# Expert blocks in four 32-column tiles, turns on VectorE, gather behind scatter: a four-layer mixer stack with a mixture of experts

## Chip, cores and metric

One NeuronCore of a Trainium2 chip. The metric is the device time of one launch in microseconds (us), all weights in HBM at its start. Everything is float32.

## The reference, cut to what matters

The program is a stack of mixer layers (attention, latent attention, mLSTM, a hybrid layer) over 256 tokens of width 1024, and behind them a layer of routed experts. Only that last layer is touched by the change:

```python
def clamped_swiglu(hgu):
    gate, up = jnp.split(hgu, 2, axis=-1)
    gate = jnp.minimum(gate, SWIGLU_LIMIT)
    up = jnp.clip(up, -SWIGLU_LIMIT, SWIGLU_LIMIT)
    return gate * jax.nn.sigmoid(SWIGLU_ALPHA * gate) * (up + 1)

# routed_moe: 256 tokens, 32 experts, top 4 of them for each token
top_v, top_e = lax.top_k(xt @ w_router + b_router, TOP_K)
gates = jax.nn.softmax(top_v, axis=-1)
# the 1024 assignments are sorted by expert; each expert gets blocks of 64 slots
def expert_block(args):
    xb, e = args                                  # 64 x 1024
    return clamped_swiglu(xb @ w1[e] + b1[e]) @ w2[e] + b2[e]   # w1: 1024x2048, w2: 1024x1024
# y[token] += gate * yb[slot];  x = x + gate2 * y;  the output is rms_norm(x, final_norm_w)
```

## The kernel before

The experts' weights are 12 MB each: eight chunks of 1 MB of w1 (128 input features each, c = 0 to 7) and four of w2 (c = 8 to 11). `expert_weights` in SBUF holds exactly 12 chunks. SyncE (SP) issues all loads (L2066): chunk c of the next expert goes out when the semaphore `used` says that the last block of the present expert is done with its chunk c. Ahead of chunk 0 goes the load of the next expert's bias (`load_bias1`, L2795), which waits for `bias_used` of that last block.

An expert with more than 64 assignments has two or more blocks. There are 36 blocks for 32 experts; a plan, made on VectorE while block 0 runs (`sort_and_plan`), orders the experts, and the blocks from 3 on are a hardware loop (`Fori`) on each engine.

One block i on PE (TensorE): `first_products` (L3060) multiplies the 64 gathered rows `xt` with w1, gate half into PSUM bank 4 and up half into bank 5. The 64 slots fill 64 of the array's 128 columns, so two tiles run side by side, g = 0 on output features 0 to 511 and g = 1 on 512 to 1023. After chunk 3 stands the gather of block i+1 (`gather`, L3032: a matrix `pick` of ones times the normalised tokens `htok`, into bank 6). Then `scatter_last` (L3045): the output of block i-1, `ys`, times `spread`, which holds the gates by token, is added to the sums in banks 0 to 3. Then `second_products`: four transposes of the activation on PE (L3098), four of the gathered rows (`turn_gathered`, L3040), a wait for ScalarE's copy `at_` (L2923), and the products with w2 (L3108) into bank 7. Each matmul call is two matmul instructions, each with a weight load, in the trace; a transpose is one.

ScalarE (ACT): `copy_gathered` (L2900), `sigmoid` (L2919), the copy of the turned activation (L2923), and `copy_turned`, eight activations that apply the layer's scale and shift and write `xt` (L2906).

VectorE (DVE) in one block: `activation` (L3312 to L3319), `gates_of_slots` (L3325, `eq2`: which slot is which token, times its gate; L3329), `lay_bias` (four shuffles, L3183) for block i+1, `spread_slots` (L3332, a sum over 128x1024), `tables` (L3243 to L3248, the `pick` of a later block), and `outputs` (L3337), which copies bank 7 to `ys` and waits for the end of the second products.

At the end PE scatters the last block (two calls, one for each half of the tokens), and ScalarE and VectorE normalise and scale (L2938, L3370) before the stores.

## Time and profile before

| | |
|---|---|
| time, three runs | 2301.73, 2302.03, 2305.65 us (median 2302.03) |
| profiled execution | span 2306.2 us; of what lies around the span the page tells nothing |
| PE busy | 2209.2 us, 96% |
| VectorE busy | 1194.8 us, 52% |
| ScalarE busy | 650.0 us, 28% |
| read from HBM | 567.46 MB |
| TensorE clock, mean | 0.993 of full speed |

Busy PE time is the time in which at least one matmul is under way; matmuls overlap, and a matmul in another tile of the array runs at the same time. The chain of waits follows the last instruction back to what released it; a transfer is in it with the whole time from its issue to its landing, queueing behind other transfers included. The expert layer runs from about 1310 us to the end.

### The profile page before, as it was taken

To read this page: it belongs to the slowest core of one execution; us is meant where nothing else is said; L and a number is where in the kernel's file an instruction comes from. 1 tells how busy PE (TensorE), PEld (TensorE's weight loads), DVE (VectorE), ACT (ScalarE), POOL (GpSimd) and SP (SyncE) were. 2 spreads that over 40 slices of the span, in tenths; PEclk is the share of its full clock that TensorE was granted. 3 is DMA by queue.
4 is the path that set the end of the run, shared out by engine and by line. 5 is a ranking of instruction groups with operands and counts; after the bars stand their busy time and mean duration, and the time that the engine had idled before them with its cause. 6 is when DMAs were issued, how large, how long until landed. Compare 5 with 4: busy or idle time off the path is not lost. (4 is left out here: it accounts for less than half of the span.)

```text
span 2306.2 us, 29645 instructions
## 1 busy us (share of the span) xinstructions
PE 2209.2 (96%) x10363; PEld 1188.4 (52%) x10364; DVE 1194.8 (52%) x2716; ACT 650.0 (28%) x1658; POOL 101.8 (4%) x234
## 2 busy tenths in 40 slices
PE   8999899999999999999999899999999999999997
PEld 3546685478744578777878633333333323333332
DVE  4989468453895563636745453334343333334334
ACT  3018442443221363336333321111111111111112
POOL 0001000000000051002001000000000000000000
PEclk9999999999999999999999999999999999999999
DMA  9670035301477103331241599989989998998998
GB/s 398 250 291 34 1 146 191 110 1 45 175 266 278 39 2 110 110 110 38 74 147 37 231 373 421 421 357 421 422 365 422 421 421 366 421 421 366 421 421 335
DMA packets 110280, 569.68 MB, mean 247 GB/s; under 512 B 11857, under 2 KB 13649, under 8 KB 51441
## 3 DMA queue, kind: packets, MB, share of 16 engines
q1 hardware_dynamic: 110192, 568.54, 61.6%
q8 instruction: 52, 0.85, 0.2%
q14 instruction: 36, 0.29, 0.0%
HBM read 567.46 MB, written 1.05 MB: 247 GB/s over the span
## 5 line engine op out<-in xcount | busy, mean ns | idle before, releaser
L3060 PE MATMUL PS<-BIG,PW 128*64 128x512 f32 x2304 | 514.1, 594 | 15.3 <-DMA BIG<-in_w 14.7
L3060 PEld LDWEIGHTS PS<-BIG,PW 128*64 128x64 f32 x2304 | 161.6, 137 | 353.6 <-issue 301.9
L3312 DVE TENSOR_SCALAR PW<-PS 128x512 f32<-128x512 f32 x36 | 24.9, 692 | 494.6 <-PE PS L3060 494.6
L3108 PE MATMUL PS<-BIG,PW 128*64 128x512 f32 x1152 | 255.4, 595 | 8.6 <-ACT PW L2923 8.6
L386 DVE SCALAR_TENSOR_TENSOR BIG<-BIG,COND_ROWS 128x1024 f32<-128x1024 f32 x128 | 153.4, 1221 | 24.9 <-DMA BIG<-in_w_ada_columns 24.6
L3108 PEld LDWEIGHTS PS<-BIG,PW 128*64 128x64 f32 x1152 | 79.2, 137 | 161.0 <-issue 142.7
L2900 ACT COPY BIG<-PS 128x512 f32<-128x512 f32 x37 | 21.7, 586 | 486.6 <-PE PS L3032 486.6
L1148 PE MATMUL PS<-HT,BIG 128*128 128x512 f32 (+1 forms) x448 | 152.0, 501 | 0.0
L1148 PEld LDWEIGHTS PS<-HT,BIG 128*128 128x128 f32 x448 | 85.1, 190 | 65.3 <-issue 60.3
L658 PE MATMUL PS<-HT,BIG 128*128 128x256 f32 x512 | 111.6, 379 | 1.4 <-PEq L863 1.4
L1553 PE MATMUL PS<-BIG,HT 128*128 128x512 f32 x256 | 110.0, 592 | 0.0
L658 PEld LDWEIGHTS PS<-HT,BIG 128*128 128x128 f32 x512 | 97.1, 190 | 14.9 <-issue 1.8
L386 DVE SCALAR_TENSOR_TENSOR PW<-BIG,COND_ROWS 128x1024 f32<-128x1024 f32 x80 | 97.5, 1219 | 11.4 <-ACT COND_ROWS L1169 5.0
L2906 ACT ACTIVATE PW<-PS,MOD,GAIN 128x64 f32<-128x64 f32 x296 | 91.9, 423 | 0.7 <-PE PS L3040 0.7
L2919 ACT ACTIVATE PW<-PW 128x512 f32<-128x512 f32 x36 | 22.7, 630 | 225.6 <-DVE PW L3312 225.1
L993 DVE TENSOR_REDUCE ST<-PS 128x2 f32<-128x1024 f32 (+1 forms) x64 | 65.5, 1023 | 34.8 <-PE PS L1413 32.2
L1553 PEld LDWEIGHTS PS<-BIG,HT 128*128 128x128 f32 x256 | 48.6, 190 | 61.2 <-issue 61.2
L924 ACT ACTIVATE PW<-PS,ST 128x512 f32<-128x512 f32 (+1 forms) x128 | 77.3, 615 | 9.3 <-DVE ST L999 4.8
L3045 PE MATMUL PS<-PW,HT 64*128 64x512 f32 x288 | 72.9, 625 | 0.9 <-DVE PW L3337 0.9
L886 PE MATMUL PS<-CONST,PW 128*128 128x128 f32 x416 | 61.2, 286 | 11.4 <-DVE PW L1012 11.4
L937 ACT COPY PW<-PS 128x512 f32<-128x512 f32 (+1 forms) x128 | 58.7, 509 | 44.2 <-PE PS L886 43.6
L3032 PE MATMUL PS<-BIG,HT 128*64 128x512 f32 x296 | 69.9, 593 | 1.0 <-DVE HT L3237 1.0
(547 smaller groups left out, 3171.6 us busy)
## 6 DMA issues: line engine op xcount, KB each, us to landing
BIG<-in_w SPq DMA_DIRECT2D x384, 1024.0 KB, 16.1
BIG<-in_l_w_ada_columns SPq DMA_DIRECT2D x40, 1024.0 KB, 7.2
BIG<-in_l_w_in SPq DMA_DIRECT2D x19, 2048.0 KB, 8.5
BIG<-in_w_ada_columns SPq DMA_DIRECT2D x24, 1024.0 KB, 7.1
BIG<-in_l_w_out SPq DMA_DIRECT2D x8, 2048.0 KB, 8.5
BIG<-in_w_in SPq DMA_DIRECT2D x7, 2048.0 KB, 8.1
BIG<-in_l_w_ada SPq DMA_DIRECT2D x4, 2048.0 KB, 17.9
BIG<-in_w_out SPq DMA_DIRECT2D x2, 2048.0 KB, 7.8
```

The lines of the kernel that those rows point to most:

```text
L386: ins = nc.vector.scalar_tensor_tensor(w if s else PRODUCTS, w, 1.0, COND_ROWS[:, row, :], ALU.mult, ALU.mult, accum_out=modulation(l)[:, ...
L658: ins = nc.tensor.matmul(PS[:, j % 4, 0:LAT], w[:, k, (m % 4) * P:(m % 4 + 1) * P], ot[:, k, s * LAT:(s + 1) * LAT], start=(k == 0), stop= ...
L886: ins = nc.tensor.transpose(PS[:, 4 + h, j * P:(j + 1) * P], probs[:, i % 2, h, kt * P:(kt + 1) * P], ident)
L924: nc.scalar.activation(probs[:, i % 2, h, a:b], PS[:, 2 * (i % 2) + h, a:b], ACT.Exp, bias=nm[:, i % 2, h:h + 1], scale=scale, accum_out=d ...
L993: dve_chain.link(dve, nc.vector.tensor_reduce(mx[:, i % 2, 0:2], s[:, :, a:b], AX, ALU.max))
L1148: ins = nc.tensor.matmul(PS[:, j % 4, 0:tok], *ops, start=(k == 0), stop=(k == KT - 1))
L1553: ins = nc.tensor.matmul(o, HT[:, k, m[1] * P:(m[1] + 1) * P], w[:, k, :], start=(k == 0), stop=(k == KT - 1))
L2906: nc.scalar.activation(xt[:, k % 4, k // 4, :], turned[:, k % 4, k // 4, :], ACT.Identity, bias=shift[:, k, :], scale=gained[:, k, :]).the ...
L3032: ins = nc.tensor.matmul(PS[64 * g:64 * g + 64, 6, :], pick[:, a, :], htok[:, a, g * 512:g * 512 + 512], start=(a == 0), stop=(a == 1))
L3045: ins = nc.tensor.matmul(PS[:, 2 * a + g, :], spread[64 * g:64 * g + 64, a * P:(a + 1) * P], ys[64 * g:64 * g + 64, :], start=False, stop= ...
L3060: ins = nc.tensor.matmul(PS[64 * g:64 * g + 64, 4 + half, :], xt[:, c % 4, c // 4, :], W[:, c, half * F + g * 512:half * F + g * 512 + 512 ...
L3108: ins = nc.tensor.matmul(PS[64 * g:64 * g + 64, 7, :], at_[:, k % 4, k // 4, :], W[:, 8 + k // 2, k % 2 * D + g * 512:k % 2 * D + g * 512 ...
```

## The change

A block keeps its 64 slots but is worked on as two parts u = 0, 1 of 32 slots. A part fills 32 columns, so four tiles run side by side, each with 256 output features; a chunk and half takes eight matmul calls of 256 columns where it took two of 512. Gather and second products are cut in the same way. The scatter becomes four row tiles of 32 slots. The output sums in banks 0 to 3 are laid out by feature quarter for it, and the two scatters at the end signal once, after the second.

The activation and the gathered rows are turned by VectorE (`nc.vector.transpose`, which turns each 32x32 block) in place of eight PE transposes and two ScalarE copies. The gather moves from inside the first products to behind the scatter. Since `spread` needs the two parts apart, VectorE does `eq2` and the sum over 128x1024 twice in each block; its `turn_gathered` stands ahead of them, and in front of the sort in block 0. The bias row for an expert is 8 KB in place of 16.

```diff
                     def scatter(a):
-                        for g in range(2):
-                            ins = nc.tensor.matmul(PS[:, 2 * a + g, :], spread[64 * g:64 * g + 64, a * P:(a + 1) * P],
-                                                   ys[64 * g:64 * g + 64, :], start=False, stop=False, skip_group_check=True)
+                        for u in range(2):
+                            for g in range(4):
+                                ins = nc.tensor.matmul(PS[:, g, a * 256:a * 256 + 256], spread[rows_of(g), u, a * P:(a + 1) * P],
+                                                       ys[rows_of(g), u * 256:u * 256 + 256], start=False, stop=False, tile_position=(PART * g, 0),
+                                                       skip_group_check=True)
                         return ins
...
                             for half in range(2):
-                                for g in range(2):
-                                    ins = nc.tensor.matmul(PS[64 * g:64 * g + 64, 4 + half, :], xt[:, c % 4, c // 4, :],
-                                                           W[:, c, half * F + g * 512:half * F + g * 512 + 512], start=False, stop=(c == 7),
-                                                           skip_group_check=True)
+                                columns = W[:, c, half * F:half * F + F].rearrange("p (k q x) -> p k q x", q=4, x=64)
+                                for u in range(2):
+                                    for g in range(4):
+                                        ins = nc.tensor.matmul(part_of(4 + half, g, u).rearrange("p (k x) -> p k x", x=64), xt[:, u, c, :],
+                                                               columns[:, :, g, :], start=False, stop=(c == 7), tile_position=(0, PART * g),
+                                                               skip_group_check=True)
...
                     def second_products(i, load, beside=None):
-                        pe.wait_ge(loop["act_ready"], i + 1)
-                        for j in range(4):
-                            cols = slice(j // 2 * 2 * P + j % 2, (j // 2 + 1) * 2 * P, 2)
-                            ins = nc.tensor.transpose(PS[:, 7, j * P:(j + 1) * P], act_[:, cols], ident)
-                        ins.then_inc(loop["act_turned"], 1)
-                        turn_gathered(i + 1)
-                        pe.wait_ge(loop["act_copied"], i + 1)
+                        pe.wait_ge(loop["act_turned"], i + 1)
...
                     with pe.Fori(3, n) as i:
                         load = pe.value_load(plan[0:1, bass.ds(i, 1)], min_val=0, max_val=E - 1)
-                        products_and_gather(i, load)
+                        first_products(i, load)
                         scatter_last(i)
+                        gather_next(i)
                         second_products(i, load)
                     pe.wait_ge(loop["spread_ready"], n)
                     pe.wait_ge(loop["y_copied"], n)
-                    for a in range(2):
-                        scatter(a).then_inc(ending["tile_scattered"], 1)
+                    scatter(0)
+                    scatter(1).then_inc(ending["tiles_scattered"], 1)
...
+                    def turn_gathered(i):
+                        dve.wait_ge(loop["gathered"], i + 1)
+                        nc.vector.transpose(xturned, PS[:, 6, :].rearrange("p (u k r) -> p u k r", u=2, r=PART)).then_inc(loop["gather_turned"], 1)
+
...
                     ts(first_blocks, blocks[:, 0:1], -1.0, None, ALU.add).then_inc(loop["first_blocks_ready"], 1)
+                    turn_gathered(0)
...
                         nc.vector.scalar_tensor_tensor(act_, up, 1.0, sig, ALU.add, ALU.mult).then_inc(loop["act_ready"], 1)
+                        dve.wait_ge(loop["act_ready"], i + 1)
+                        nc.vector.transpose(at_.rearrange("p u (k j) s -> p (u k) j s", j=2), act_.rearrange("p (k r j) -> p k j r", r=PART, j=2)).then_inc(loop["act_turned"], 1)
...
+                    def spread_slots(i):
+                        dve.wait_ge(steps, i * 10 + 7)
+                        nc.vector.tensor_reduce(spread[:, 0, :], eq2.rearrange("p k t -> p t k"), AX, ALU.add).then_inc(steps, 1)
+                        dve.wait_ge(steps, i * 10 + 8)
+                        gates_of_slots(1)
+                        dve.wait_ge(steps, i * 10 + 9)
+                        nc.vector.tensor_reduce(spread[:, 1, :], eq2.rearrange("p k t -> p t k"), AX, ALU.add).then_inc(loop["spread_ready"], 1)
                         nc.vector.tensor_scalar(slot, slot, float(SLOT), None, ALU.add).then_inc(steps, 1)
...
                     with dve.Fori(1, n) as i:
                         activation(i)
-                        gates_of_slots(i, load_of(i + 1))
+                        load = load_of(i + 1)
+                        turn_gathered(i + 1)
+                        dve.wait_ge(bias_landed, load * 16 + 16)
+                        gates_of_slots(0)
                         lay_bias()
                         dve.wait_ge(loop["scattered"], i)
-                        spread_slots()
-                        dve.wait_ge(loop["gathered"], i + 2)
-                        tables(lambda x: i * 8 + (8 + x))
+                        spread_slots(i)
+                        tables(lambda x: i * 10 + (10 + x))
                         outputs(i)
```

In the code before block 1's loop, `turn_gathered(1)` stands behind VectorE's four copies of `drow` and `grow` (L3347) and ahead of `gates_of_slots(0)` and `lay_bias()`.

## Rows read from the trace of the kernel before

**Rows 1.** The page's chain that ended last, by engine.

```profile
PE 31%; DMA 7%; DVE 3%; SPq 2%; ACT 1%; issue 1%; ACTq 0%; DVEq 0%
```

**Rows 2.** Windows: us, busy us (instructions) of each engine, PEclk, DMA share, GB/s.

```profile
1926.00:2102.00 176.00, 169.89 (x792) 58.75 (x790) 63.23 (x134) 27.14 (x71) 0.00 (x0) 1.00 1.01 421
2102.00:2114.00 12.00, 12.00 (x58) 3.98 (x57) 5.73 (x14) 2.14 (x8) 0.00 (x0) 1.00 0.44 156
```

**Rows 3.** Chain that ended last, 1820 to 2306: start us, us, what.

```profile
1909.29 1.96 PE PS L3060 x8
...
2096.33 1.96 PE PS L3060 x8
...
2101.81 7.09 PE PS L3108 x32
```

**Rows 4.** SP: two loads in time order; waits of its queue (total, times, longest).

```profile
1359.84 22.71 SPq L2066 DMA_DIRECT2D BIG<-in_w  x12
...
2110.81 24.67 SPq L2066 DMA_DIRECT2D BIG<-in_w  x12
...
SPq L2795 <- DVE PS L3183: 81.1, 4, 22.2
```

**Rows 5.** Timeline of PE near the program's start: four 32-column tiles.

```profile
34.87 1.94 PE L314 MATMUL PS<-BIG,COND 128*32 128x256 f32 x32
```

**Rows 6.** Timeline of one block in the loop, PE and DVE.

```profile
1533.06 1.99 PE L3045 MATMUL PS<-PW,HT 64*128 64x512 f32 x8
...
1534.51 0.69 DVE L3319 SCALAR_TENSOR_TENSOR PW<-PW 128x512 f32<-128x512 f32 x1
...
1536.67 7.09 PE L3108 MATMUL PS<-BIG,PW 128*64 128x512 f32 x32 [0.24 <-ACT PW L2923]
...
1543.59 7.04 PE L3060 MATMUL PS<-BIG,PW 128*64 128x512 f32 x32
```

**Rows 7.** Groups by form, DVE, 1510 to 2280: busy us, mean ns | idle before.

```profile
L3183 DVE STREAM_SHUFFLE PS<-BIG 128x256 f32<-128x256 f32 x116 | 41.8, 423 | 0.0
L3325 DVE SCALAR_TENSOR_TENSOR HT<-HT,SM 128x1024 f32<-128x1024 f32 x29 | 37.2, 1284 | 2.1
```

**Rows 8.** PE's sequencer at a loop top: ns min/median/max, first and last start us.

```profile
L3165 PEldq ALU_OP  x1: 32/32/32, 1539.3 to 1539.3; - x1
...
L3057 PEldq FUSED_REGOPS  x1: 37/37/37, 1540.7 to 1540.7; - x1
```

**Rows 9.** Timeline of block 0, 1318 to 1347.

```profile
1321.97 0.15 DVE L3256 TENSOR_SCALAR SM<-SM 128x1 int32<-128x1 f32 x1
...
1323.07 0.59 ACT L2900 COPY BIG<-PS 128x512 f32<-128x512 f32 x1 [3.11 <-PE PS L3032]
...
1326.78 0.43 PE L3123 MATMUL PS<-PW,CONST 32*128 32x64 f32 x2
...
1346.81 3.65 PE L3108 MATMUL PS<-BIG,PW 128*64 128x512 f32 x16 [0.24 <-ACT PW L2923]
```

**Rows 10.** Timeline of the last block and the ending.

```profile
2290.25 1.94 DVE L3332 TENSOR_REDUCE HT<-HT 128x256 f32<-128x1024 f32 x1
...
2293.48 0.58 DVE L3248 TENSOR_REDUCE HT<-PW 128x64 f32<-128x256 f32 x1
2295.94 0.69 DVE L3337 TENSOR_TENSOR PW<-PS,BIG 128x512 f32<-128x512 f32 x1 [1.87 <-PE PS L3108]
2296.78 1.99 PE L3045 MATMUL PS<-PW,HT 64*128 64x512 f32 x8 [0.89 <-DVE PW L3337]
2297.94 0.60 ACT L2938 ACTIVATE PW<-PS 128x512 f32<-128x512 f32 x1 [5.30 <-PE PS L3045]
```

**Rows 11.** DMA by queue: of 1500 to 2290, of all; issues with us to landing.

```profile
q1 hardware_dynamic: 44626, 319.54, 97.6%
...
q8 instruction: 52, 0.85, 0.2%
...
out<-BIG SPq DMA_DIRECT2D x4, 256.0 KB, 2.2
```

More of the change, by code:

```diff
@@ L3106, in second_products @@
                                 pe.wait_ge(chunk_landed[8 + k // 2], load * 16 + 16)
-                            for g in range(2):
-                                ins = nc.tensor.matmul(PS[64 * g:64 * g + 64, 7, :], at_[:, k % 4, k // 4, :],
-                                                       W[:, 8 + k // 2, k % 2 * D + g * 512:k % 2 * D + g * 512 + 512], start=(k == 0),
-                                                       stop=(k == KT - 1))
+                            for u in range(2):
+                                for g in range(4):
+                                    ins = nc.tensor.matmul(part_of(7, g, u), at_[:, u, k, :],
+                                                           W[:, 8 + k // 2, k % 2 * D + g * 256:k % 2 * D + g * 256 + 256],
+                                                           start=(k == 0 and u == 0), stop=(k == KT - 1), tile_position=(0, PART * g),
+                                                           skip_group_check=True)
                             if k % 2 == 1:
@@ L3150, in _ @@
                     load = pe.value_load(plan[0:1, 1:2], min_val=0, max_val=E - 1)
-                    products_and_gather(1, load)
+                    first_products(1, load)
                     scatter_last(1)
+                    gather_next(1)
                     second_products(1, load)
                     load = pe.value_load(plan[0:1, 2:3], min_val=0, max_val=E - 1)
-                    products_and_gather(2, load)
+                    first_products(2, load)
                     pe.wait_ge(loop["bias2_scaled"], 1)
                     for a in range(2):
-                        for g in range(2):
-                            nc.tensor.matmul(PS[:, 2 * a + g, :], gates_by[0:E, a * P:(a + 1) * P], bias2[0:E, g * 512:g * 512 + 512],
-                                             start=False, stop=False, skip_group_check=True)
+                        for g in range(4):
+                            ins = nc.tensor.matmul(PS[:, g, a * 256:a * 256 + 256], gates_by[0:E, a * P:(a + 1) * P], bias2[0:E, g * 256:g * 256 + 256],
+                                                   start=False, stop=False, skip_group_check=True)
+                    ins.then_inc(loop["bias2_added"], 1)
+                    pe.wait_ge(loop["bias2_added"], 1)
                     scatter_last(2)
+                    gather_next(2)
                     second_products(2, load)
@@ L3306, in _ @@
                                                 ALU.add).then_inc(loop["gates_spread"], 1)
-                    dve.wait_ge(loop["gathered"], 1)
                     tables(lambda x: x)
@@ L3321, in load_of, with gates_of_slots @@
                     def load_of(i):
                         return dve.value_load(plan[0:1, bass.ds(i, 1)], min_val=0, max_val=E - 1)
-                    def gates_of_slots(i, load=None):
-                        nc.vector.scalar_tensor_tensor(eq2, drow, slot, grow, ALU.is_equal, ALU.mult).then_inc(steps, 1)
-                        dve.wait_ge(steps, i * 8 + 7)
-                        if load is not None:
-                            dve.wait_ge(bias_landed, load * 16 + 16)
+                    def gates_of_slots(u):
+                        nc.vector.scalar_tensor_tensor(eq2, drow, slot[:, u:u + 1], grow, ALU.is_equal, ALU.mult).then_inc(steps, 1)
@@ L3347, in _ @@
                             nc.vector.tensor_copy(flat(dst[:, 2 * h:2 * h + 2, :]), PS[:, 4 + h, :]).then_inc(loop["places_copied"], 1)
+                    turn_gathered(1)
                     dve.wait_ge(loop["places_copied"], 4)
+                    gates_of_slots(0)
                     lay_bias()
-                    gates_of_slots(0)
-                    spread_slots()
+                    spread_slots(0)
                     dve.wait_ge(loop["gains_copied"], 2)
                     outputs(0)
-                    dve.wait_ge(loop["gathered"], 2)
-                    tables(lambda x: 8 + x)
+                    tables(lambda x: 10 + x)
                     dve.wait_ge(*at("late_loaded", 32))
```

108 lines of the change are left out of this document (50 added, 58 removed).

## The prediction

> **What bounds the kernel now.** I read the page's chain of waits first. It puts 31% of the span on PE and 7% on DMA [rows 1], so a reader would look to TensorE. The windows say otherwise for the expert loop. Over 1926 to 2102 the 16 DMA engines are full (share 1.01, 421 GB/s), and behind it lies a short hole (2102 to 2114 at 0.44) [rows 2]. There are four such holes, one where an expert needs two blocks: there SP also waits for VectorE before the bias load, four times [rows 4]. The two blocks of such an expert use one set of weights, so no slot of the 12 MB ring comes free until the second block has used its chunk 0.
>
> A cycle from hole to hole is 7 blocks and 6 experts: chunk 0 of A, the first block of a two-block expert, is past when PE waits for its chunk 7, at 2096.33, and the matching point of the cycle before is 1909.29, 187.0 us earlier [rows 3]. Six experts are 6 x 12 x 1.049 MB = 75.5 MB, at 421 GB/s 179.3 us; the other 7.7 us are the hole. PE's own period is 26.1 us a block (first products to first products), 182.6 for seven: PE has 4.4 us a cycle to spare, 0.6 a block, and beyond 187.0 / 7 = 26.7 us a block it would become the bound. So work taken off PE is given back as waiting for chunks. What counts is three places: the hole, the start of the stream, and the tail after the last chunk.
>
> **The hole, before.** PE waits for chunk 7 of A (landing at x = 2096.33), multiplies it in 1.96, and starts the second products at 2101.81, x + 5.48. They take 7.09; then chunk 0 of block B is multiplied and SP issues the next load at 2110.81, x + 14.5 [rows 3, 4]. All of that is in front of the DMA's restart.
>
> **The change on that path.** (1) *Matmuls.* A two-tile pair moves 2 x 512 columns, four tiles 4 x 256: equal work. Eight two-tile matmuls of a chunk take 1.96 [rows 3]; 32 four-tile ones of 256 columns, a form the kernel already has at its start, take 1.94 for the work of a chunk [rows 5]. So first products 13.8, gather 1.8 and second products 7.0 stay as they are, at 0.054 us a matmul where it was 0.22. The scatter as four row tiles of 32 is shown nowhere. Two row tiles of 64 run at full overlap (8 in 1.99) [rows 6], so I take 1.84 and keep 3.5 (two at a time) as the other end.
>
> The Trainium skill (TensorE: Matmul & The Clock Gate, Back-to-back issue gap) gives about 81 ns a matmul as the sustained floor of load and matmul pairs at 128 columns. By it the 448 matmuls of a block would take 36 us and not 24. The trace's row, 61 ns each with the tail of the last one in it, does not bear it out for four tiles.
>
> (2) *Order.* Before, scatter (1533.06), wait, four turns of the activation, four of the gathered rows, ACT's copy, second products at 1536.67: 3.6 us from scatter to second products [rows 6]. After: scatter 1.84, gather 1.84, 3.7 us together. Beside it VectorE ends its last product at 1535.20 and turns it; the turn of 128x512 is bounded by a 128x512 product (0.69) and by a 128x1024 strided sum scaled to 512 (1.94 in [rows 10], half is 0.97) [rows 6]. I take 0.69: the shuffle, the nearest operation, takes 0.42 for 256 columns [rows 7]. Ready at 1536.0 or 1536.3, before PE comes at 1536.8. So the four turns, the copy and their waits leave PE (some 1.8 us a block), the gather takes their place, and second products start 0.1 later relative to x: 4 x 0.1 = +0.4 over four holes. In the plain blocks PE's period falls from 26.1 to about 24.5, and that buys nothing.
>
> (3) *Loop top.* PE's sequencer does the branch, the read of the expert number and the waits from 1539.3 to 1540.7, 1.4 us, while PE still has work up to 1543.59 [rows 6, 8]. That lead, 4.3 us, is some 19 matmuls and their loads at 0.22. After the change 19 matmuls last 19 x 0.054 = 1.05. If the lead is a number of instructions, PE idles 1.4 - 1.05 = 0.4 at each loop top, one of which lies in each hole: 4 x 0.4 = +1.6. Bounds: 0 (a deeper queue), and 1.4 each, 5.6 (no lead).
>
> (4) *Bias.* Its load halves to 8 KB; for the second block it has landed, and xt and the bias are ready about 3.5 us after the second products begin, against 7: hidden. The cover gone, each us late would cost as much in each hole.
>
> **The start.** Block 0 [rows 9]: the gather's ACT copy (from 1323.07) and the four turns become one VectorE turn, so block 0 starts some 0.6 earlier. But `turn_gathered(0)` stands in front of the sort on VectorE and waits for the gather (its queue is free at 1322.1, the gather ends at 1323.05, the turn 0.7 later): the sort comes 1.7 later. PE asks for it at 1326.78 only, after chunk 0, so part of that is free; I leave 0.9 as delay, between none and the whole 1.7. Before the second products of block 0 (1346.81) turns and copy are gone, as in every block: of the 1.8 there I count 1.4 here, since less PE work stands between. Net -0.5. The stream becomes full when SP issues chunk 0 of expert 2 at 1359.84 [rows 4], 3.9 after the end of these second products, and moves with them: -0.5. Block 1 waits for `turn_gathered(1)`, which stands behind four copies on VectorE, some 0.9 us; its chunk 0 is done at 1358.5, before SP asks. Bounds -1.5 and +1.5 (the sort's delay kept whole). ACT's eight row copies of 256 for four of 512 end 0.3 later, in front of nothing.
>
> **The tail.** After the last chunk nothing hides anything. Before, VectorE was done with its tables at 2294.06, and `outputs` started when PE ended, 2295.94 [rows 10], 7.14 after the second products began. After, VectorE waits for the gather (S + 0.25, S the start of the second products), and then has in front of `outputs`: turn 0.65, eq2 1.2, four shuffles 1.35, sum 1.94, eq2 1.42, sum 1.94, slot 0.1, tables 1.95 [rows 7, 10] = 10.55. `outputs` starts at S + 10.7, not 7.14: +3.5. (In other blocks y is needed only at the next scatter, S + 21: hidden.) Then the ending waits for both scatters and not one: 1.16 from the scatter's start to ACT's first square before [rows 10], 2.05 after: +0.9. Tail +4.4; the bounds are 3.9, and 5.5 with the slow turn twice and a slower scatter's 1.6 apart.
>
> **Sum.** -0.5 + 0.4 + 1.6 + 4.4 = +5.9. The page gives 2306.2 as span of the profiled execution, 4.2 over the median of the runs, 2302.03; from 2306.2 the sum is 2312.1, and I carry the difference to the median: 2307.9, say 2308. A change under 0.2%, 4.6 us, is about what cannot be told from none.
>
> **Rivals.**
> *No idle at the loop top, no change.* The queue is deep enough, or the start gives 1.5: +3 to +4.3, 2305 to 2306.3, within 0.2%. For it: the lead is seen only in time, not as a count. 0.24.
>
> *PE was the bound after all, faster.* The chain's 31% on PE [rows 1] would then be real and 1.1 to 1.6 us a block be saved: 33 x 1.1 = -36, 2270. Against it stands a DMA share of 1.01 over 170 us at a stretch. Together with smaller gains in the holes (a scatter and gather that overlap): 0.09.
>
> *The loop outgrows instruction memory, clearly slower.* PE's loop has 248 instructions now (64, 32, 8 and 8 matmuls, 112 in all, as many loads, turns, control) and about 920 after (448 matmuls). In the loop before, the only queue that moves is the data's; in the whole program instruction packets of queue 8 number 52, of 0.85 MB, 16 KB each [rows 11]. If a branch back then waits for such a packet, the smallest transfers land in 2.2 us [rows 11]: 4 x 2.2 = 9 in the holes, and PE's period 24.9 + 2.2 = 27.1 passes 26.7, where it becomes the bound: 0.4 x 33 = 13 more instead of idle. About +20 to +25, 2325 to 2330. Below a stall of 1.8 only the holes pay. How many such packets PE keeps, no row shows. The Trainium skill (Runtime: NRT & Kernel Launch, Instruction fetch mechanics) speaks both ways: 128 KiB for PE, which would hold the loop, and a window of two 16 KiB pages outside of which a taken branch stalls. With it goes the case that four-tile matmuls in long runs take more than 60 ns each (26.7 us / 448), from which point PE decides too: at 70 ns a block takes 31.4, and 4.7 x 33 = 155 us are added. Both together 0.10.
>
> *Main case*, 2306.7 to 2316 (the latter with the slow scatter, 1.6 in four holes and in the tail): 0.57.
>
> **Numbers.** Slower 0.57 + 0.10 = 0.67; within 0.2% 0.24; faster 0.09. Range 2302 to 2316: it leaves out the faster case and the fetch case; the main case's own range is 2306.7 to 2312.
>
> **What would show it.** In the loop: DMA share still 1.01 between four holes, holes 0.5 longer; L3060's successor in 13.8 a block; PE idle 0.4 at the loop top; more PE idle on DMA in the last two or three blocks of a cycle; second products 5.5 after chunk 7. In the tail: `outputs` 10.7 after the second products began. Wrong it would be if VectorE turns cost over 1.5 us, if instruction packets appear after 1450 us, or if a block exceeds 26.7.

## The result: 0.28% slower, and the profile after

Median of the changed kernel 2311.97 us against 2306.36 us of the kernel before, 20 runs each in turns; ratio 1.0028, 95% interval 1.0021 to 1.0034, which is +6.5 us (+4.8 to +7.8). Forecast was 1.0026, +5.9 us, as 2308 against the 2302.03 that three runs had given; with 20 runs the kernel before stands at 2306.36. The profiled execution took 2313.27 us with a span of 2311.5.

The page's chain by engine, where [rows 1] gave PE 31% and DMA 7%:

```profile
PE 27%; DMA 11%; SPq 4%; issue 1%; DVE 1%; ACT 0%; ACTq 0%; DVEq 0%
```

Its instruction queue (packets, MB, share), against 52 packets in [rows 11], and its group of the first products (busy us, mean ns | idle before, and what ended most of it), with that of the kernel before under it:

```profile
q8 instruction: 63, 1.03, 0.2%
...
L3061 PE MATMUL PS<-BIG,PW 128*32 128x256 f32 x9216 | 527.2, 381 | 53.6 <-DMA BIG<-in_w 48.0
```

```profile
L3060 PE MATMUL PS<-BIG,PW 128*64 128x512 f32 x2304 | 514.1, 594 | 15.3 <-DMA BIG<-in_w 14.7
```

The chain that ended last, around the hole that answers to [rows 3] (start us, us, what):

```profile
1909.15 1.93 PE PS L3061 x32
...
2096.36 1.93 PE PS L3061 x32
2098.30 1.94 PE PS L3043 x32
2100.24 1.86 PE PS L3035 x32
2102.10 6.91 PE PS L3097 x128
2109.01 14.02 PE PS L3061 x256
...
2126.83 6.91 PE PS L3097 x128
```

SP's first load behind this hole (2110.81 in [rows 4]), and a window of the loop in front of it (columns as in [rows 2]):

```profile
2111.16 23.11 SPq L2066 DMA_DIRECT2D BIG<-in_w  x12
```

```profile
1969.90:2099.90 130.00, 119.78 (x2108) 68.43 (x2096) 65.43 (x113) 14.19 (x37) 0.00 (x0) 1.00 1.01 422
```

What is to be seen: PE takes the last chunk (chunk 7 of the first block A) at x = 2096.36, and from there scatter (L3043), gather (L3035), second products (L3097) and the next block's first products stand end to end. The second products start at x + 5.74, where it was x + 5.48 in [rows 3]. A block takes 24.73 us from second products to second products (2102.10 to 2126.83), 26.1 before, and yet a cycle from hole to hole is as long as it was: 187.2 us (1909.15 to 2096.36) against 187.0. The DMA engines are full (1.01, 422 GB/s), and PE now waits 48.0 us in all for chunks, 14.7 before. (That x itself lies within 0.03 of [rows 3] is chance: this execution reached block 0's gather 2.9 us earlier and lost 2.4 us there to a low clock.)

VectorE in the last block (the timeline: start us, us, what), where [rows 10] had `outputs` at 2295.94, that is x + 12.62 with x = 2283.32 (first row, of the kernel before):

```profile
2283.32 1.96 PE PS L3060 x8
```

```profile
2288.71 0.72 DVE L3236 STREAM_TRANSPOSE BIG<-PS 128x512 f32<-128x512 f32 x1 [1.04 <-PE PS L3035]
2289.35 1.24 DVE L3325 SCALAR_TENSOR_TENSOR HT<-HT,SM 128x1024 f32<-128x1024 f32 x1
...
2291.87 2.04 DVE L3329 TENSOR_REDUCE HT<-HT 128x256 f32<-128x1024 f32 x1
2293.94 1.28 DVE L3325 SCALAR_TENSOR_TENSOR HT<-HT,SM 128x1024 f32<-128x1024 f32 x1
2295.26 1.89 DVE L3333 TENSOR_REDUCE HT<-HT 128x256 f32<-128x1024 f32 x1
...
2298.98 0.68 DVE L3339 TENSOR_TENSOR PW<-PS,BIG 128x512 f32<-128x512 f32 x1
```

Here x is 2282.90 (chain), so `outputs` (L3339) starts at x + 16.08, 3.46 later than before. VectorE had work without a gap from 2288.71; the list of that work is the delay. Then the chain of the ending, and the windows beside it (us, busy us of each engine, PEclk, DMA share, GB/s):

```profile
2299.81 3.27 PE PS L3043 x32
2303.10 0.70 DVE BIG L3376
```

```profile
2296.00:2299.80 3.80, 0.00 (x0) 0.02 (x1) 3.63 (x8) 0.00 (x0) 0.00 (x0) 1.00 0.00 0
2299.80:2303.10 3.30, 3.25 (x32) 2.54 (x32) 0.00 (x0) 0.00 (x0) 0.00 (x0) 0.59 0.00 0
2303.10:2311.50 8.40, 0.00 (x0) 0.00 (x0) 4.07 (x10) 4.46 (x12) 0.00 (x0) 0.50 0.33 125
```

The scatter that takes 1.94 in the loop takes 3.27 here, at a granted clock of 0.59: most of it at the lower level, 1.2 GHz. PE had nothing to do for 4.3 us before it. In that wait the clock still stood at 1.00, and so it did from 2299.80 to 2300.30, in the first part of the scatter; from 2301.00 on it is 0.50. From x to the end of the span the changed kernel needs 28.6 us (2282.90 to 2311.5), the kernel before 22.9 (2283.32 to 2306.2): +5.7, nearly the whole difference.

### The profile page after: what moved, and what is told of

It is laid out like the page before. It is cut to its first block and busy times, and to the rows that moved or that the text cites. A ratio compares the mean times of both kernels' runs of the same rounds, so it can differ in the third digit from the quotient of the medians.

```text
span 2311.5 us, 53432 instructions
## 1 busy us (share of the span) xinstructions
PE 2186.8 (95%) x22199; PEld 1398.5 (61%) x22200; DVE 1360.3 (59%) x2861; ACT 622.2 (27%) x1591; POOL 101.7 (4%) x234
## 5 line engine op out<-in xcount | busy, mean ns | idle before, releaser
L3061 PE MATMUL PS<-BIG,PW 128*32 128x256 f32 x9216 | 527.2, 381 | 53.6 <-DMA BIG<-in_w 48.0
L3061 PEld LDWEIGHTS PS<-BIG,PW 128*32 128x32 f32 x9216 | 292.8, 110 | 286.0 <-DMA BIG<-in_w 102.7
L3097 PE MATMUL PS<-BIG,PW 128*32 128x256 f32 x4608 | 255.5, 379 | 0.0
L3097 PEld LDWEIGHTS PS<-BIG,PW 128*32 128x32 f32 x4608 | 149.6, 110 | 99.2 <-DVE PW L3319 0.4
L386 DVE SCALAR_TENSOR_TENSOR BIG<-BIG,COND_ROWS 128x1024 f32<-128x1024 f32 x128 | 153.3, 1220 | 24.2 <-DMA BIG<-in_w_ada_columns 23.9
L2909 ACT ACTIVATE PW<-BIG,MOD,GAIN 128x64 f32<-128x64 f32 x296 | 102.2, 428 | 160.4 <-DVE BIG L3236 160.4
L3325 DVE SCALAR_TENSOR_TENSOR HT<-HT,SM 128x1024 f32<-128x1024 f32 x72 | 91.6, 1273 | 45.9 <-DMA BIG<-in_b_rows 44.6
L3043 PE MATMUL PS<-PW,HT 32*128 32x256 f32 x1152 | 73.6, 392 | 4.3 <-DVE PW L3339 4.3
L886 PEld LDWEIGHTS PS<-CONST,PW 128*128 128x128 f32 x416 | 45.8, 144 | 49.7 <-DVE PW L1012 44.7
L3035 PE MATMUL PS<-BIG,HT 128*32 128x256 f32 x1184 | 73.3, 389 | 1.0 <-DVE HT L3231 1.0
L3333 DVE TENSOR_REDUCE HT<-HT 128x256 f32<-128x1024 f32 x36 | 72.0, 2001 | 1.2
```

The costliest lines, as they stand in the source:

```text
L386: ins = nc.vector.scalar_tensor_tensor(w if s else PRODUCTS, w, 1.0, COND_ROWS[:, row, :], ALU.mult, ALU.mult, accum_out=modulation(l)[:, ...
L2909: nc.scalar.activation(xt[:, :, k, :], xturned[:, :, k, :], ACT.Identity, bias=shift[:, k, :], scale=gained[:, k, :]).then_inc(loop["xt_co ...
L3035: ins = nc.tensor.matmul(part_of(6, g, u).rearrange("p (k r) -> p k r", r=PART), pick[:, a, u * PART:u * PART + PART], features, start=(a ...
L3043: ins = nc.tensor.matmul(PS[:, g, a * 256:a * 256 + 256], spread[rows_of(g), u, a * P:(a + 1) * P], ys[rows_of(g), u * 256:u * 256 + 256], ...
L3061: ins = nc.tensor.matmul(part_of(4 + half, g, u).rearrange("p (k x) -> p k x", x=64), xt[:, u, c, :], columns[:, :, g, :], start=False, st ...
L3097: ins = nc.tensor.matmul(part_of(7, g, u), at_[:, u, k, :], W[:, 8 + k // 2, k % 2 * D + g * 256:k % 2 * D + g * 256 + 256], start=(k == 0 ...
```

## The experiments

Twelve kernels ran; ratios are to the kernel before. All edits are to the changed kernel unless said otherwise. In the traces, x is the start of chunk 7 of A at the fourth hole, S the start of the second products, R the first packet of the restarted stream (0.97 us behind SP's load: 2112.13 for the 2111.16 above, 2111.78 for the 2110.81 of the kernel before).

### The tail: is it VectorE's list?

**e1_y_first.**

```diff
-                        tables(lambda x: i * 10 + (10 + x))
                         outputs(i)
+                        tables(lambda x: i * 10 + (10 + x))
```

> The changed kernel, with one edit: on VectorE the copy of the block's result (`outputs`) stands ahead of `tables` in the loop. In the changed kernel's trace `outputs` of the last block starts at 2298.98, behind tables of about 1.9 us, while the second products ended at 2295.6. Theory (the tail is VectorE's list of work, every instruction ahead of `outputs` counts in full): `outputs` starts 1.9 earlier, the end comes 1.9 earlier, ratio to the changed kernel 0.9992, to the kernel before 1.0020. If PE's clock falls because it waits 4.1 us in front of the last scatter, the wait shrinks to about 2.3 and the scatter may take 2.0 instead of 3.3: then 3.1 earlier, 1.0014. Rival (tables are hidden, something else ends late, such as ScalarE or the stores): no change, 1.0028.

Measured: 1.0023 (1.0014 to 1.0033), median 2311.74. The times alone do not part this from 1.0028. The trace does (last block, x = 2280.58):

```profile
2294.80 0.68 DVE L3339 TENSOR_TENSOR PW<-PS,BIG 128x512 f32<-128x512 f32 x1
...
2295.63 2.81 PE L3043 MATMUL PS<-PW,HT 32*128 32x256 f32 x32 [2.40 <-DVE PW L3339]
```

`outputs` starts at x + 14.22, 1.86 earlier; PE waits 2.40 us and the scatter takes 2.81. From x to the end: 26.2 (2280.58 to 2306.8) against 28.6, so -2.4: 1.9 of the list and 0.5 of the scatter. The tables were on the path in full.

**e2_warm.**

```diff
+                    pe.wait_ge(loop["gather_turned"], n + 1)
+                    for m in range(32):
+                        g = m % 4
+                        nc.tensor.matmul(part_of(6, g, m // 4 % 2), ident[:, g * PART:g * PART + PART],
+                                         htok[:, 0, g * 256:g * 256 + 256], start=(m < 4), stop=True,
+                                         tile_position=(0, PART * g), skip_group_check=True)
                     pe.wait_ge(loop["spread_ready"], n)
                     pe.wait_ge(loop["y_copied"], n)
```

> The changed kernel with 32 more matmul calls on PE behind the last block's second products, into bank 6 that nobody reads any more, once in the program: about 3.6 us of PE work in the 4.1 us in which PE waits for `outputs`. It computes nothing that is used. Theory (the last scatter takes 3.3 instead of 1.94 us because the granted clock falls to half while PE waits): the clock stays at 1.00 up to the scatter, the scatter takes 1.9 to 2.1, and the end comes 1.2 us earlier; in rounds that is 0.05%, at the edge of what can be told, so the trace decides: last scatter's duration and the clock of the window before it. Rival (four row tiles of 32 slots run slower when all operands are fresh, or the scatter waits for something else): the scatter keeps 3.3 us with the clock at 1.00.

Measured: 1.0024 (1.0013 to 1.0035). PE at the end:

```profile
2293.34 3.64 PE L3167 MATMUL PS<-BIG,CONST 128*32 128x256 f32 x64
2297.96 2.01 PE L3043 MATMUL PS<-PW,HT 32*128 32x256 f32 x32 [0.98 <-DVE PW L3344]
```

With work in the gap the scatter takes 2.01 at a clock of 1.00, and x to end is 27.5 (2280.87 to 2308.4), 1.1 less. So 1.1 to 1.3 us of the tail are the clock. Where it falls varies: in the changed kernel some 0.6 us into the scatter, in e1 about 1.1 us into it (1.00 up to 2296.50, 0.50 from 2297.00 on), in e3 and e9 while PE still waits, and there the scatter took 3.65 and 3.83. So the 1.2 us of the changed kernel are one execution's share. The Trainium skill (TensorE: Matmul & The Clock Gate, Part 1) describes this as a gate whose default is the lower level, released by activity. The trace agrees in this: with 3.64 us of work in the gap the scatter ran at 1.00 and took 2.01 us, without it at 0.59 and 3.27 us.

### The hole: who sets the start of the second products?

**e3_gather_back.**

```diff
-                        first_products(i, load)
+                        products_and_gather(i, load)
                         scatter_last(i)
-                        gather_next(i)
                         second_products(i, load)
```

(`products_and_gather` is that of the kernel before; blocks 1 and 2 likewise.)

> The changed kernel with the gather of the next block back behind chunk 3 of the first products, as before; all else as changed. In the changed kernel scatter 1.94 and gather 1.86 stand between chunk 7 and the second products, which start at x + 5.6 to 5.7, x being the point at which PE gets chunk 7. Theory A (PE's list of work sets this start): it moves ahead until VectorE's turned activation is ready, about x + 4.9 by the trace (activation turned some 0.8 before PE comes), so 0.75 in each of four holes and in the tail; in the tail VectorE's turn of the gathered rows no longer waits for the gather, so `outputs` comes about 1.0 earlier in sum. Total 4 us, ratio to the kernel before 1.0010. Rival B (VectorE's activation sets the start and PE's place of the gather is free): no change, 1.0028.

Measured: 1.0013 (1.0005 to 1.0022), median 2309.8: theory A's 1.0010 is inside the interval, rival B's 1.0028 is not. PE at the same hole (x = 2089.90):

```profile
2089.90 1.93 PE L3061 MATMUL PS<-BIG,PW 128*32 128x256 f32 x32 [0.55 <-DMA BIG<-in_w]
2091.77 2.01 PE L3043 MATMUL PS<-PW,HT 32*128 32x256 f32 x32
2094.72 7.11 PE L3104 MATMUL PS<-BIG,PW 128*32 128x256 f32 x128 [0.94 <-DVE PW L3323]
```

S = x + 4.82, now set by VectorE (0.94 of waiting for its turn); R is x + 15.00 (2104.90), against x + 15.77 (2112.13) in the changed kernel and x + 15.45 (2111.78) in the kernel before. So the late gather cost 0.92 at S and 0.77 at R, and the change without it would have shortened each hole by 0.45. The tail was 28.0 (2275.88 to 2303.9), only 0.6 shorter: the last scatter there fell to the low clock as well and took 3.65.

**e6_before_gather_late**, an edit of the kernel before: its gather moved behind the scatter, nothing else.

```diff
-                        products_and_gather(i, load)
+                        first_products(i, load)
                         scatter_last(i)
+                        gather_next(i)
                         second_products(i, load)
```

> The kernel before with one part of the change alone: the gather stands behind the scatter, outside the first products; turns stay on PE, two 64-slot tiles. Theory (what stands between chunk 7 and the loads' restart counts in full, what is hidden does not): in the kernel before, scatter, waits, four turns of the activation, four of the gathered rows and the copy lie there; the gather's 1.84 us comes on top, minus what it covers of the wait for the activation (VectorE ends 0.1 to 0.3 after the scatter); the turn of the gathered rows then also waits for it. Second products start 1.3 to 1.8 later, in four holes and the tail: +6.5 to +9, ratio 1.003 to 1.004. Rival (the gather only changes places inside PE's work and is free): 1.000.

Measured: 1.0499 (1.0484 to 1.0514), median 2421.5. Both theories missed by over 100 us. ScalarE and PE in one block of it:

```profile
1553.76 0.59 ACT L2900 COPY BIG<-PS 128x512 f32<-128x512 f32 x1 [23.88 <-PE PS L3032]
1554.24 0.63 ACT L2919 ACTIVATE PW<-PW 128x512 f32<-128x512 f32 x1
```

```profile
1526.14 0.74 PE L3098 MATMUL PS<-CONST,PW 128*128 128x128 f32 x4 [2.74 <-DVE PW L3322]
...
1527.56 8.64 PE L3108 MATMUL PS<-BIG,PW 128*64 128x512 f32 x32 [0.24 <-ACT PW L2923]
```

In the kernel before, ScalarE copies the gathered rows (L2900) ahead of the sigmoid (L2919). With the gather late, the sigmoid stood behind a copy that waited for PE's gather; VectorE waited for the sigmoid, PE 2.74 us for VectorE, and its next products took 8.64 in place of 7.09, because the clock fell (0.64 in the window 1527.50 to 1532.00). A block took 30.3 us, beyond the 26.7 at which PE decides: 33 x 3.6 = 119.

**e10_before_late_ordered**: the same, and in ScalarE's loop

```diff
-                        copy_gathered(i + 1)
                         sigmoid(i)
+                        copy_gathered(i + 1)
                         copies(i)
```

> The kernel before with the gather moved behind the scatter, as in the run that came out 115 us longer, but with ScalarE's copy of the gathered rows behind the sigmoid and not ahead of it. Theory (those 115 us came from ScalarE's queue: the copy waits for the late gather, the sigmoid stands behind it, and VectorE and PE wait for the sigmoid, 4.3 us a block): without it the second products start at about x + 7.2 (gather to x + 3.9, then turn, copy, turn) and not x + 5.5; a block stays at 26.2 to 26.4 us; +1.7 in four holes and in the tail, +8.5, ratio 1.0035. Rival (the late gather itself costs, by its own place on PE or by the clock): ratio above 1.03 still.

Measured: 1.0036 (1.0024 to 1.0049), median 2313.55; x = 2100.50 and S = 2107.58, x + 7.08, R = x + 17.05 (2117.55), 1.6 later than before. As expected. So the late gather alone costs the kernel before as much as the whole change; and it is only bearable with the ScalarE copy out of the way. In the change that copy is gone, and VectorE's turn of the gathered rows stands where nothing urgent is behind it, except in the last block.

### What PE has to spare, and where

**e4_pe_plus1 and e5_pe_plus2.** In the loop, behind chunk 1 (in e5 behind chunks 1 and 2), 16 more matmul calls into bank 6, which the gather overwrites:

```diff
+                    def more_work(c):
+                        if c in (1,):
+                            for m in range(16):
+                                g = m % 4
+                                nc.tensor.matmul(part_of(6, g, m // 4 % 2), xt[:, 0, 0, :], htok[:, 0, g * 256:g * 256 + 256],
+                                                 start=(m < 4), stop=True, tile_position=(0, PART * g), skip_group_check=True)
-                        first_products(i, load)
+                        first_products(i, load, beside=more_work)
```

> The changed kernel with 16 more matmul calls in each block of the loop, behind chunk 1 of the first products, into bank 6 (their result is overwritten by the gather). About 1.8 us of PE work a block, in front of the point where PE waits for chunk 7. Theory (the stream of weights is the bound while PE's own period stays below 187.0 / 7 = 26.7 us): the period goes from 24.7 to 26.5, all of it is taken from PE's waiting for chunks, and the time stays within 0.05% of the changed kernel, 1.0028 of the kernel before. Rival (PE's chain of waits is real): 33 blocks x 1.8 = +60 us, ratio 1.029.

> As the kernel with 16 more calls behind chunk 1, and 16 more behind chunk 2: 3.7 us of PE work a block more than in the changed kernel. Theory: PE's period goes to 28.4 us, 1.7 above 26.7, and PE becomes the bound: 33 x 1.7 = +56 us against the changed kernel, ratio to the kernel before about 1.027, with an idle share of the DMA engines in the loop. Rival 1 (the stream is the bound whatever PE does): 1.003. Rival 2 (PE's chain is real): +33 x 3.7 = 120 us, 1.055.

Measured: e4 1.0051 (1.0037 to 1.0065), e5 1.0226 (1.0202 to 1.025), median 2356.12. e5 is as its theory has it: +46 us against 56 expected; (28.15 - 26.71) x 33 = 47.5 with the block as its chain has it (second products at 2078.34 and 2106.49) and 187.0 / 7 = 26.71. The forecast had taken 1.8 us for the added work; it measures 1.73. No wait for a chunk is on its chain from 1900 to 2140. e4 came out 5 us above the changed kernel, where nothing was expected. The 10 us behind the restart, first the changed kernel's, then e4's (windows, columns as above):

```profile
1924.90:1929.90 5.00, 5.00 (x100) 3.13 (x95) 1.18 (x3) 0.00 (x0) 0.00 (x0) 1.00 0.95 324
1929.90:1934.90 5.00, 5.00 (x100) 3.10 (x92) 0.00 (x0) 0.00 (x0) 0.00 (x0) 1.00 1.00 416
```

```profile
1928.50:1933.50 5.00, 5.00 (x100) 3.13 (x95) 1.20 (x3) 0.00 (x0) 0.00 (x0) 1.00 0.88 313
1933.50:1938.50 5.00, 5.00 (x100) 3.10 (x92) 0.00 (x0) 0.00 (x0) 0.00 (x0) 1.00 0.95 377
```

The stream restarts when PE frees chunk 0 and then needs each further chunk freed in time; the added work holds back chunk 2. These rows explain 0.6 us a hole ((324 + 416 - 313 - 377) GB/s x 5 us / 421 GB/s), about half; the cycle up to the fourth hole is 188.5 us in e4 and 187.2 in the changed kernel. That the added work is the reason for the thinner stream is argued from its place, and tested only by e9 and e11.

**e9_pe_plus1_late** and **e11_pe_plus1_mid**: the same 16 calls behind chunk 6 and behind chunk 4 (`if c == 6`, `if c == 4`).

> The changed kernel with 16 more matmul calls in each block (1.73 us), behind chunk 6 of the first products and not behind chunk 1. The kernel with them behind chunk 1 came out 5 to 6 us longer than the changed one, where nothing was expected; its trace shows the stream thinner in the first 10 us after each restart (313 and 377 GB/s against 324 and 416). Theory (work between the chunks that the restarting stream needs first counts; the same work behind chunk 6 is hidden): time as the changed kernel, ratio 1.0028, within 1 us. Rival (at a block of 26.4 us PE is simply too near to its limit of 26.7, wherever the work stands): ratio 1.005 again.

> The changed kernel with the 16 more matmul calls a block (1.73 us) behind chunk 4 of the first products. Behind chunk 1 they gave 1.0051 and behind chunk 6 1.0063. Two readings. A (the place counts): behind chunk 1 they are late for the restarting stream; behind chunk 6 they stand after the wait for chunk 6, and chunk 7, which lands 2.5 us later, finds PE 1.2 us late. Behind chunk 4 the stream has 0.76 of slack from each chunk before (2.49 us to land, 1.73 to multiply) and PE has the slack of chunks 5 to 7 to catch up (3 x 0.76 = 2.3 against 1.73): nothing is added, ratio 1.003. B (a block of 26.4 us is too near to 26.7, wherever the work stands): 1.005 to 1.006 again.

Measured: behind chunk 6 1.0063 (1.0047 to 1.0078), behind chunk 4 1.0025 (1.0013 to 1.0036). The theory for chunk 6 fell. Its trace shows why: PE waits for chunk 6, and what is behind that wait is on the path.

```profile
2094.74 1.93 PE L3061 MATMUL PS<-BIG,PW 128*32 128x256 f32 x32 [0.54 <-DMA BIG<-in_w]
2096.49 1.91 PE L3162 MATMUL PS<-BIG,PW 128*32 128x256 f32 x32
2098.22 1.91 PE L3061 MATMUL PS<-BIG,PW 128*32 128x256 f32 x32
```

Chunk 7 lands 2.5 us after chunk 6 (the waits of this run are 2.47 to 2.50 apart), so PE comes 1.0 late to it (2098.22 and not 2097.2), in four holes and the tail. That is 5 of the 8 us between this ratio and that of the changed kernel (intervals of 3 us each way); the last scatter is 0.6 longer as well (3.83 for 3.27), and for the rest I have no row. Behind chunk 4 the same work costs nothing. So the reading "the place counts" stands, and "a block of 26.4 is too near to 26.7" falls: with 1.73 us more in every block the stream still sets the time.

### Versions that take the costs out

**e7b_all.** Gather back as in e3, `outputs` ahead of `tables` as in e1, and the first product of slots and places for the next block at the end of the present one:

```diff
                         dve.wait_ge(bias_landed, load * 16 + 16)
-                        gates_of_slots(0)
+                        nc.vector.tensor_copy(tmp[:, 0:1], ones[:, 0:1])
                         lay_bias()
...
                         spread_slots(i)
+                        outputs(i)
                         tables(lambda x: i * 10 + (10 + x))
-                        outputs(i)
+                        dve.wait_ge(loop["spread_ready"], i + 1)
+                        gates_of_slots(0)
```

> The changed kernel with three edits together: gather back behind chunk 3; `outputs` ahead of `tables`; and the first product of slots and places (`gates_of_slots(0)`, 1.28 us on VectorE) computed for the next block at the end of the present one instead of between turn and shuffles (with a one-column copy in its place). Theory (hole and tail are lists of work, each piece counts in full): holes 4 x 0.75 = 3.0; tail 0.7 from the gather, 1.9 from tables, 1.3 from the product, 1.2 from PE's clock kept, but not more than down to the end of the second products (2295.6 against `outputs` at 2299.0, so 3.4 for `outputs` in all), 4.6 with the clock. Sum 7 to 8 us less than the changed kernel: about 1 to 2 below the kernel before, ratio 0.9993 to 0.9997. Rival (a further chain, on ScalarE or the stores, stands behind these): it stays above 1.001.

Measured: 0.9995 (0.9983 to 1.0008), median 2305.89: 7.6 us under the changed kernel by the ratios, no difference from the kernel before. x to end is 24.2 (2283.08 to 2307.3). In its chain the ending waits for tables and product, which had moved behind `outputs`:

```profile
2295.46 0.59 DVE PW L3343
2296.05 0.68 DVE PW L3245 x2
...
2297.93 1.19 DVE HT L3329
2299.12 0.61 DVE BIG L3385
```

**e8_staged.** Gather back; `spread` is made at the head of VectorE's loop, where it waited some 10 us, and copied into place later:

```diff
                     with dve.Fori(1, n) as i:
+                        stage_spread(i)
                         activation(i)
                         load = load_of(i + 1)
                         turn_gathered(i + 1)
                         dve.wait_ge(bias_landed, load * 16 + 16)
-                        gates_of_slots(0)
-                        lay_bias()
                         dve.wait_ge(loop["scattered"], i)
-                        spread_slots(i)
+                        nc.vector.tensor_copy(spread, staged).then_inc(loop["spread_ready"], 1)
+                        lay_bias()
```

(`stage_spread` is eq2, sum, eq2, sum into `staged`, and the step of `slot`.)

> The changed kernel with the gather back behind chunk 3, and VectorE's four instructions that make `spread` (two products, two sums, 6.7 us) moved to the head of the loop, where VectorE waits some 10 us for the first products; they write to a spare place, and between turn and shuffles a copy of 128x512 brings the result to `spread`. The ending still waits for both scatters. Theory (hole and tail are lists of work): second products at x + 4.8, so the stream restarts 0.45 earlier than in the kernel before and 0.75 earlier than in the changed one, in each of four holes; in the tail `outputs` is set by the end of the second products again, x + 12, PE waits for one us only and keeps its clock, the scatter takes 1.95 and the end comes at x + 23 (22.9 in the kernel before, 28.6 in the changed one). Sum against the changed kernel -3.0 - 5.6 = -8.6, ratio to the kernel before 0.9990. Rival (VectorE becomes late somewhere in the loop, because 6.7 us now stand ahead of the clip of the gate half): holes or blocks grow and the ratio is above 1.000.

Measured: 0.9996 (0.9986 to 1.0007), median 2304.39. The last block in its chain (x = 2277.29; span 2300.6):

```profile
2282.11 7.16 PE PS L3105 x128
2289.29 0.70 DVE PW L3355
2290.13 2.04 PE PS L3044 x32
```

`outputs` starts with the end of the second products, the scatter takes 2.04, x to end is 23.3, and at the fourth hole (x = 2090.86) R is x + 15.04: tail and hole as expected. The ratio is 0.06% above the expected 0.9990, within its interval.

**e12_staged_turn_in_sort**: e8, and `turn_gathered(0)` behind the scan of `light_rank` in the sort.

> The kernel with the gather back and `spread` made at the head of VectorE's loop, and one more edit: in block 0 VectorE's turn of the gathered rows stands behind the two scans of the sort and not in front of the sort. In that kernel's trace VectorE waits 0.97 us for the gather in front of this turn, and PE then waits 1.21 us for the sort in front of its first sorting product (0.99 us of it would be gone). Theory: block 0 ends up to 0.97 earlier and the stream of the second expert starts as much earlier; ratio to the kernel before 0.9992. Rival (block 0's end is set by something else, such as the landing of its weights): 0.9996 as without this edit.

Measured: 0.9974 (0.9962 to 0.9986), median 2303.63 against 2308.12: faster than the kernel before, and by its ratio the best of all. In block 0 the turn no longer holds the sort up, and the first sorting product (L3120) stands at once behind chunk 0. The start in the kernel before (its gather; the rest in [rows 9]), in e8 (PE, with SP's first chunk of expert 2 as last row) and here:

```profile
1321.09 1.94 PE L3032 MATMUL PS<-BIG,HT 128*64 128x512 f32 x8 [0.99 <-DVE HT L3237]
```

```profile
1318.62 1.93 PE L3036 MATMUL PS<-BIG,HT 128*32 128x256 f32 x32 [0.99 <-DVE HT L3236]
...
1325.05 0.43 PE L3120 MATMUL PS<-PW,CONST 32*128 32x64 f32 x2 [1.21 <-DVE PW L3276]
...
1343.74 3.66 PE L3105 MATMUL PS<-BIG,PW 128*32 128x256 f32 x64
...
1353.81 7.11 PE L3062 MATMUL PS<-BIG,PW 128*32 128x256 f32 x128 [0.90 <-ACT PW L2910]
...
1357.19 4.27 SPq L2066 DMA_DIRECT2D BIG<-in_w  x4
```

```profile
1316.83 1.93 PE L3036 MATMUL PS<-BIG,HT 128*32 128x256 f32 x32 [0.99 <-DVE HT L3236]
...
1322.22 0.43 PE L3120 MATMUL PS<-PW,CONST 32*128 32x64 f32 x2
...
1340.91 3.66 PE L3105 MATMUL PS<-BIG,PW 128*32 128x256 f32 x64
```

From gather to second products of block 0: 25.12 in e8, 24.08 here; from gather to SP's first chunk of expert 2: 38.57 in e8, 37.55 here (1354.38). That is 1.0 us, as expected; the ratios show 5 us between the two kernels (0.22%). What the other 4 us are no trace shows: x to R (15.01) and x to end (23.3) are those of e8, and in the profiled executions gather to end takes 983.3 us here and 982.0 in e8. One thing on record bears on it. Here the kernel before ran at a mean granted clock of 0.9932 and e12 at 0.9957, where for e8 it was 0.9944 and 0.9943; and among the 20 runs of the kernel before, a mean clock lower by 0.001 goes with 1.3 us more. By that about 3 us of e12's 6 us go with the clock, and whether the edit has a part in it is open. From the parts I would put this version 2.5 us under the kernel before (0.2 + 1.0 in the start, 4 x 0.43 in the holes, less 0.4 in the tail), 0.9989, outside the interval. So an advantage is shown, its size is not.

## Why the prediction was right, point by point

**The bound.** Right. The stream sets the loop and PE's shorter blocks are given back (48.0 us of waiting for chunks in the page's group above, 14.7 before; DMA share 1.01 in the loop). e4, e11 and e5 put the limit where the sum had it, 26.7 us a block: 26.4 is free in the right place, 28.2 is not. What the prediction left out is that the spare time is not the same at every point of a block.

**Matmuls.** Right: 128 second-product matmuls in 6.91, 54 ns each, and the scatter as four row tiles in 1.94, next to full overlap; the bound of 3.5 fell. The Trainium skill's 81 ns a matmul at 128 columns (TensorE: Matmul & The Clock Gate, Back-to-back issue gap) is not borne out by four column tiles at 256 columns: 54 ns for each.

**Order.** Right in kind, too small in size: +0.1 was forecast for S, +0.26 measured. From x to SP's first load it is 14.77, 14.75, 14.75 and 14.80 in the four holes, 14.47 or 14.48 before: +1.2 in all and not +0.4. The three pieces in front of S are 1.93, 1.94 and 1.86, where I had 1.84 for the last two. VectorE's turn costs 0.71, as taken (0.69). The whole stretch cannot confirm the 1.2: from x of the first hole to x of the last block the kernel before and the changed one both take 778.2 us in their profiled executions, and e2, whose holes are the same, takes 779.5.

**Loop top.** Wrong: +1.6 was forecast, none came. PE's sequencer starts the branch at 2107.6 and is through at 2108.8, while PE has work up to 2109.01 (chain above). The lead did fall, as argued, from 4.3 us to 1.4, but it is some 26 matmuls at 0.054 and not 19, and 1.4 just covers the 1.2 that the sequencer needs. By luck the error of this term and that of the order nearly cancel (2.0 forecast, 1.2 measured).

**Start.** Right for block 0, wrong for the stream: -0.5 was forecast for both. From the gather to the second products of block 0 it takes 25.72 before ([rows 9] have the second at 1346.81) and 25.12 with the change, e1, e2, e3 and e8 alike: -0.6. But SP's first chunk of expert 2 did not move with them. Block 1 waits 0.9 us for ScalarE's rows (last block of rows of e8 above), which stand behind VectorE's copies and `turn_gathered(1)`: its products start 35.19 after the gather, 34.71 before, and SP issues the chunk 38.57 after it, 38.75 before: -0.2. At x of the first hole nothing is left of it: 184.0 us after the gather before, 184.1 to 184.6 in e1, e2, e3 and e8. The forecast saw this wait and took it as hidden. PE's wait for the sort was 1.21 (0.9 taken), and e12 shows that it was avoidable. In the profiled execution of the changed kernel itself the clock was 0.50 from 1317.5 to 1327.7, which hides all this.

**Tail.** +4.4 forecast, +5.7 measured. `outputs` is later by 3.46, from VectorE's list as e1 and e8 show: 3.2 counted from S (3.5 forecast), and 0.3 because S itself is later, which the forecast had counted in the holes but not here. Both scatters awaited, 0.9: no run measures it apart, but e8 has it, whose tail is 0.4 above that of the kernel before while S is 0.66 earlier, so about 1.0. Missing was the clock: 1.1 to 1.3 more, shown by e2. The term was mis-sized by that.

**Sum.** -0.2 + 1.2 + 5.7 = +6.7, against +6.5 from the ratio. That the forecast's +5.9 is so near is in part luck: 1.6 us of idle at the loop top never came, and 0.3 in the start, 0.8 in the holes and 1.3 in the tail had been left out. What was right is the mechanism: the stream is the bound, PE's savings come back as waiting, and the tail is VectorE's list.

**Rivals**: "PE was the bound" fell (e4, e11, and the chain). "No idle at the loop top, no change" had its condition met and its result not, since tail and order took more. The fetch rival fell: 63 instruction packets and not 52, all of them before 1440 us, though the loop grew to some 920 instructions; none is fetched in the loop. (Its price of 2.2 us a packet was read from stores of 256 KB, which are not the smallest transfers.) That the scatter alone would be slow fell too.

## What to carry to other kernels

Where a stream of weights sets the time, look for the stretches in which it stands still (holes, start, tail) and count each engine's list of work there, the last block's above all; what an edit saves elsewhere comes back as waiting. Follow a saving up to the load that restarts the stream: 0.6 us saved in block 0 was 0.2 there. Work is free only where both sides have slack: not behind the last landing that PE waits for, and not in front of the chunks that a restarting stream needs first. When a producer is moved later, look in every queue for what stands behind the consumer's wait: here that decided between +8 and +115 us.

## What was not expected of the hardware

- Behind a wait of 4.3 us on PE 32 small matmuls took 3.27 in place of 1.94 to 2.01 us (clock 0.59), behind one of 2.40 us 2.81, and behind 0.91 to 0.98 us 2.01. In the first two the clock stood at 1.00 through the wait and fell some 0.6 and 1.1 us into the matmuls; in e9 it fell in the wait, and they took 3.83. In e6 2.74 us of waiting a block made second products 8.64 in place of 7.09.
- PE's sequencer ran 4.3 us ahead of its work with matmuls of 0.22 us and 1.4 us with matmuls of 0.054: about 19 and 26 matmuls, nearer to a fixed count than to a fixed time.
- A loop of some 920 PE instructions ran with no instruction packet in it.
- Four row tiles of 32 slots, each into a bank of its own, ran at 1.94 for 32 matmuls of 256 columns, 61 ns each.
